# Loading the turned memory and the first key weights of a two-layer trunk in alternate pieces of 2, 2 and 4 chunks

## The chip, the cores and the metric

The kernel runs on one core of one Trainium2 chip. The metric is the device time of one launch in microseconds (us), lower is better. The trace comes from one execution under the hardware profiler; times of the trace are counted from the start of its span.

## The reference

A trunk of two layers over 256 rows of width 1024, all float32. Each layer runs a mixer (HGRN2, a short convolution and latent attention beside each other), a cross attention to a memory of 256 rows, and a mixture of 32 experts. Only the keys of the cross attention matter for the change:

```python
h = h + cross_attention(rms_norm(h, norm_cross[l]), rms_norm(mem, norm_mem[l]),
                        xa_wq[l], xa_wk[l], xa_wv[l], xa_wo[l])
# in cross_attention(h, m, wq, wk, wv, wo):
k = (m @ wk).reshape(B_, m.shape[1], XA_HEADS, XA_DIM)
v = (m @ wv).reshape(B_, m.shape[1], XA_HEADS, XA_DIM)
```

The product `m @ wk` sums over a width of 1024, which the kernel cuts into 8 chunks of 128 (KC = 8).

## The kernel before, in words

The first thing that the kernel computes is the keys and values of layer 0's cross attention, since they need only `mem` and weights. The weights come from HBM as units: `xk0` to `xk3` are the four quarters of `xa_wk`, `xv0` to `xv3` those of `xa_wv`, 1 MB each. All units go in a fixed order (RING_ORDER) through six ring buffers of 2 MB, `ring[0]` to `ring[5]`. SyncE (SP) issues every one of these loads from one queue. A unit's load is issued when TensorE has freed its buffer (`unit_free`), and its landing is counted on `unit_in[slot]`. At the start all six buffers are free. The order in which SP issues at the start is written out by hand (L572 to L584):

- half the turned memory (chunks 0 to 3, into `memN`, which lies in `early[5]`), half of `xk0` (chunks 0 to 3, into `ring[0]`), the other half of the memory, the other half of `xk0`, 512 KB each;
- `xk1`, `mem` in rows (into `kT`), the tables, `xk2`, `x`, the turned `x` (into `uT`), and then `xk3`, `xv0` and on.

VectorE multiplies the turned memory by the norm's gain, two chunks at a time, from `memN` into `mT` (L1811, four instructions, counted on `mem_gained`). The first and the third wait for a half of the memory (`memT_in`). The norm's row factors are put in later: ScalarE and VectorE compute them from `mem` in rows, and TensorE spreads them over the partitions (L921, `spread_rstd`) between `xk1` and `xk2`.

TensorE first runs WARM_UP = 10 products of zeros from `states` (L926), which depend on nothing that is loaded. Then come the keys of `xk0` (L937): for each of 8 chunks two products of 128 x 256, each of which the trace shows as two MATMUL records, so 32 in all. Chunk 0 waits for `part_in[0]` (the first half of `xk0`), chunk 4 for `unit_in[0]` (the second half), and every second chunk for `mem_gained`. `xk1`, `xk2` and `xk3` follow at once (`fill_keys`, L663), then the values (L722), then the mixer's projections.

The same semaphores `part_in[0]` to `part_in[2]` are used again much later, for the halves of the three last expert units of each layer (PARTED). The waits for them are at L799 and L869.

Much later the expert stages read 2 MB units from the ring and from the early buffers. There the loads run back to back and TensorE waits for some of them.

Of the kernel before, what the change touches and what calls it, by code (L numbers as in the profile page):

```python
# [28 lines left out]
P = 128  # L29
L = 2  # L30
S = 256
D = 1024
T = S // P
KC = D // P
# [16 lines left out]
RING = 6  # L51
UNIT = 4096
LEVELS = 4
WARM_UP = 10
LEAST_BLOCK = 8
UNIT_DMAS = 1
LOADED = 16 * UNIT_DMAS
# [26 lines left out]
UNIT_AT = [0]  # L84
# [207 lines left out]
def hybrid_trunk(nc, tables, level_masks, a, out):  # L292
    with ExitStack() as ctx:
        def sb(name, shape, dt=F32, stack=ctx):
            return stack.enter_context(nc.sbuf_tensor(name, shape, dt))

        def sem(name):
            return ctx.enter_context(nc.semaphore(name))


        ring = [sb(f"ring{n}", [P, UNIT]) for n in range(RING)]
# [3 lines left out]
        h = early[4][:, 0:T * D].rearrange("p (t d) -> p t d", t=T)  # L305
# [3 lines left out]
        memN = early[5][:, 0:KC * S].rearrange("p (c s) -> p c s", c=KC)  # L309
# [120 lines left out]
        unit_in = [sem(f"unit_in{n}") for n in range(RING)]  # L430
# [6 lines left out]
        memT_in = [sem(f"memT_in{n}") for n in range(2)]  # L437
        part_in = [sem(f"part_in{n}") for n in range(len(PARTED))]
# [29 lines left out]
        fixed_units = a["fixed_units"]  # L468
# [8 lines left out]
        def _(sp):  # L477
# [92 lines left out]
                    sp.dma_start(dst, src).then_inc(unit_in[slot], 16)  # L570

            sp.wait_ge(unit_free, 1)  # L572
            first = fixed_units[0, UNIT_AT[0]:UNIT_AT[1]].rearrange("(p h x) -> p h x", p=P, h=2)
            for n in range(2):
                half = slice(n * KC // 2 * S, (n + 1) * KC // 2 * S)
                sp.dma_start(memN.rearrange("p c s -> p (c s)")[:, half], a["mem_turned"][:, half]).then_inc(memT_in[n], 16)
                sp.dma_start(ring[0][:, half], first[:, n]).then_inc(part_in[0] if n == 0 else unit_in[0], 16)
            static_unit(0, 1)
            sp.dma_start(kT.rearrange("p c s -> p (c s)").rearrange("p (t d) -> p t d", t=T),
                         a["mem"].rearrange("b (t p) d -> p (b t) d", p=P)).then_inc(mem_in, 16)  # L580
# [37 lines left out]
        def _(pe):  # L618
# [29 lines left out]
            def wait_unit(base, name, of=None):  # L648
                wait_number(base, RING_AT[lay if of is None else of, name])
# [106 lines left out]
            def unit_memory(base, n, buffer, loads):  # L756

                if buffer is None:
                    if halved(n) is not None:
                        pe.wait_ge(half_in[halved(n)], LOADED * (lay + 1))  # L760
                    wait_number(base, n)
                    return ring[n % RING]
                pe.wait_ge(early_in[buffer], LOADED * loads)
                return early[buffer]

            def freed(buffer):
                return unit_free if buffer is None else early_free
# [59 lines left out]
            def down_view(unit):  # L827

                return unit.rearrange("p (h e c x) -> p e c h x", h=2, e=QUAD, c=2)
# [33 lines left out]
            def last_quarter(E, units, j):  # L863

                q = QUADS - 1
                number, buffer, loads = units[j // 2]
                w = down_view(unit_memory(None, number, buffer, loads))
                if j % 2:
                    pe.wait_ge(part_in[1 + j // 2], LOADED * (lay + 1))  # L869
                for c in range(2):  # L870
                    for e in range(QUAD):
                        mm = pe.matmul(bank[j % 2][32 * e:32 * e + 32, 0:S], turned[:, 2 + c, 32 * e:32 * e + 32], w[:, e, c, j % 2],
                                       start=(c == 0), stop=(c == 1), tile_position=(0, 32 * e))
                    if j == 2 and c == 0:
                        pe.wait_ge(E["m_down"], q * 2 + 2)
                        pe.sem_inc(freed(units[0][1]), 1)
                mm.then_inc(E["m_down"], 1)
# [14 lines left out]
            def last_down_and_scatter(E, units):  # L892

                pe.wait_ge(E["turned"], QUADS)
                last_quarter(E, units, 0)
                if lay == L - 1:
                    keep_busy(3, 4)
                last_quarter(E, units, 1)
                add_last_quarters(E, 0)
                if lay < L - 1:  # L900
                    last_quarter(E, units, 2)
                    add_last_quarters(E, 1)
                    last_quarter(E, units, 3)
                    add_last_quarters(E, 2)
                    add_last_quarters(E, 3)
                else:
                    last_quarter(E, units, 2)
                    add_last_quarters(E, 1)
                    last_quarter(E, units, 3)
                    for t in range(T):  # L910
                        for j in (2, 3):
                            add_last_quarter(E, j, t)
# [10 lines left out]
            lay = 0  # L923
            pe.wait_ge(setup_done, 1)
            for _ in range(WARM_UP):
                pe.matmul(bank[7][:, 0:P], states[:, 0, 0], states[:, 0, 1], start=True, stop=True)  # L926
            o = begin("xk0")
            w = slot_view("xk0")
            for c in range(KC):
                if c % 2 == 0:  # L930
                    pe.wait_ge(mem_gained, c // 2 + 1)
                if c == 0:
                    pe.wait_ge(part_in[0], LOADED)
                if c == KC // 2:
                    wait_unit(0, "xk0")
                for k in range(2):
                    mm = pe.matmul(o[:, k * S:(k + 1) * S], w[:, c, k * P:(k + 1) * P], mT[:, c], start=(c == 0 and k == 0),  # L937
                                   stop=(c == KC - 1), skip_group_check=True)
# [797 lines left out]
        def _(dve):  # L1736
# [68 lines left out]
            dve.memset(states[:, :, :, :], 0.0).then_inc(setup_done, 1)  # L1805
            dve.wait_ge(params_in, 16)
            for n in range(4):
                if n % 2 == 0:
                    dve.wait_ge(memT_in[n // 2], 16)
                first_gain = ptab[:, 0, PARAMS["gains"][0] + 2 * KC + 2 * n:PARAMS["gains"][0] + 2 * KC + 2 * n + 2]  # L1810
                dve.tensor_tensor(mT[:, 2 * n:2 * n + 2], memN[:, 2 * n:2 * n + 2],  # L1811
                                  first_gain.unsqueeze(2).broadcast_to([P, 2, S]), ALU.mult).then_inc(mem_gained, 1)
# [720 lines left out]
```

## Time and profile before

| | |
|---|---|
| device time, median of 3 runs | 899.73 us |
| lowest and highest of the 3 | 899.07 and 900.69 us |
| device time of the profiled execution | 902.04 us |
| its span | 900.2 us |
| TensorE busy | 843.3 us, 94% |
| TensorE's granted clock, mean over the span | 0.987 |
| HBM read | 270.76 MB |

The span is the time from the first to the last instruction of the profiled execution; its device time is 1.8 us longer. PE stands for TensorE's products, PEld for its weight loads, which run beside them, SPq for SyncE's queue. A granted clock of 1.00 is TensorE's 2.4 GHz, 0.50 is 1.2 GHz.

### The profile page before, as it was taken

Reading aid. Unit: us, or ns where it says so; the run is one execution under the profiler, and the core shown is the slowest. Engines: PE = TensorE matmul, PEld = TensorE weight load, DVE = VectorE, ACT = ScalarE, POOL = GpSimd, SP = SyncE. Lnnn points to the kernel's source line nnn. Section 1 sums busy time; section 2 is a strip of 40 time slices with the busy share of each in tenths; the row PEclk is TensorE's granted clock in tenths of the full one; section 3 lists DMA queues with packets and bytes.
Section 4 is the critical chain, followed back from the end, with each engine's and each line's share of the span. In section 5 each row is a group of like instructions: output and inputs, shape, how many; then the busy total and the mean of one; then the engine's idle time right before and its main releaser. Section 6 shows DMA issues by size and latency. Waiting matters only on the chain.

```text
span 900.2 us, 12111 instructions
## 1 busy us (share of the span) xinstructions
PE 843.3 (94%) x5188; PEld 564.8 (63%) x5188; DVE 275.1 (31%) x571; ACT 169.4 (19%) x399; POOL 15.0 (2%) x21
## 2 busy tenths in 40 slices
PE   8999999999999999989879999999999999877776
PEld 7888876679755655535527887766975644332333
DVE  2317557132234111101104674723122421110112
ACT  1211134411222000000012112451121200000003
POOL 0600000000000000000000000000000000000000
PEclk9999999999999999999999999999999999999899
DMA  9943555074678999999999445507766899999995
GB/s 348 390 171 132 188 187 187 12 302 162 272 283 339 427 424 429 426 428 425 426 422 380 150 156 194 204 1 272 312 280 226 341 428 424 428 427 427 427 422 234
DMA packets 25944, 272.64 MB, mean 303 GB/s; under 512 B 3232, under 2 KB 3616, under 8 KB 7200
## 3 DMA queue, kind: packets, MB, share of 16 engines
q1 hardware_dynamic: 24592, 270.52, 74.0%
q10 hardware_dynamic: 1296, 1.30, 0.5%
q8 instruction: 44, 0.72, 0.3%
q14 instruction: 12, 0.10, 0.0%
HBM read 270.76 MB, written 1.05 MB: 302 GB/s over the span
## 4 chain that ended last, share of the span: by engine, by line
PE 75%; DMA 20%; ACT 1%; SPq 1%; DVE 1%; issue 1%; another core or an unknown queue 0%; PEld 0%; DVEq 0%; PEldq 0%; ACTq 0%
DMA early<-in_expert_units 19%; PE bank L663 18%; PE bank L745 12%; PE bank L801 7%; PE bank L1165 6%; PE bank L775 4%; PE bank L841 3%; PE bank L722 3%; PE bank L853 3%; PE bank L730 2%; PE bank L1195 2%; PE bank L1176 2%; PE bank L984 2%; SPq L552 1%; PE bank L937 1%; PE bank L684 1%
## 5 line engine op out<-in xcount | busy, mean ns | idle before, releaser
L663 PE MATMUL bank<-uT,ring 128*128 128x256 f32 x480 | 107.0, 381 | 1.4 <-DVE uT L1786 0.8
L663 PEld LDWEIGHTS bank<-uT,ring 128*128 128x128 f32 x480 | 90.3, 190 | 15.2 <-issue 1.4
L801 PE MATMUL bank<-ring,xT 128*32 128x512 f32 x560 | 69.1, 630 | 17.7 <-DMA ring<-in_expert_units 17.5
L801 PE MATMUL bank<-early,xT 128*32 128x512 f32 x464 | 55.1, 610 | 15.4 <-DMA early<-in_expert_units 15.3
L1165 PEld LDWEIGHTS bank<-uT,ring 128*128 128x128 f32 x512 | 57.8, 192 | 1.1 <-DVE uT L1786 0.5
L1165 PE MATMUL bank<-uT,ring 128*128 128x128 f32 x512 | 57.8, 275 | 0.0
L745 PE MATMUL bank<-ring,early 128*128 128x512 f32 x128 | 56.6, 592 | 0.0
L801 PEld LDWEIGHTS bank<-ring,xT 128*32 128x32 f32 x560 | 17.5, 113 | 61.4 <-issue 43.9
L745 PE MATMUL bank<-ring,uT 128*128 128x512 f32 x128 | 55.9, 592 | 0.0
L853 PE MATMUL bank<-yy,states 128*128 128x512 f32 x112 | 54.1, 612 | 0.0
L2275 DVE TENSOR_TENSOR hid<-hid,bank 128x256 f32<-128x256 f32 x16 | 6.7, 421 | 150.1 <-ACT hid L1659 150.1
L775 PE MATMUL bank<-sel,hn 128*128 128x128 f32 x448 | 52.3, 275 | 0.0
L775 PEld LDWEIGHTS bank<-sel,hn 128*128 128x128 f32 x448 | 51.3, 192 | 0.5 <-issue 0.5
L801 PEld LDWEIGHTS bank<-early,xT 128*32 128x32 f32 x464 | 14.3, 111 | 53.4 <-issue 39.3
L1659 ACT ACTIVATE hid<-bank 128x256 f32<-128x256 f32 x16 | 6.1, 384 | 192.9 <-PE bank L801 192.9
L745 PEld LDWEIGHTS bank<-ring,uT 128*128 128x128 f32 x128 | 24.2, 190 | 27.9 <-issue 27.7
L745 PEld LDWEIGHTS bank<-ring,early 128*128 128x128 f32 x128 | 23.5, 190 | 25.8 <-issue 25.8
L2280 DVE COPY yy<-bank 128x512 f32<-128x512 f32 x14 | 9.7, 692 | 97.1 <-PE bank L841 97.1
L853 PEld LDWEIGHTS bank<-yy,states 128*128 128x128 f32 x112 | 19.5, 193 | 28.9 <-issue 27.7
L2254 DVE TENSOR_TENSOR xT<-bank,ptab 128x512 f32<-128x512 f32 x28 | 19.4, 691 | 45.6 <-PE bank L775 45.6
L841 PE MATMUL bank<-ring,states 128*32 128x512 f32 x256 | 29.3, 596 | 0.0
L841 PE MATMUL bank<-early,states 128*32 128x512 f32 x192 | 22.2, 596 | 2.5 <-DMA early<-in_expert_units 2.5
(328 smaller groups left out, 1034.0 us busy)
## 6 DMA issues: line engine op xcount, KB each, us to landing
ring<-in_expert_units SPq DMA_DIRECT2D x47, 2048.0 KB, 22.7
early<-in_expert_units SPq DMA_DIRECT2D x37, 2048.0 KB, 26.6
ring<-in_fixed_units SPq DMA_DIRECT2D x16, 2048.0 KB, 8.1
ring<-in_fixed_units SPq DMA_DIRECT2D x24, 1024.0 KB, 18.0
early<-in_expert_units SPq DMA_DIRECT2D x12, 1024.0 KB, 37.8
ring<-in_expert_units SPq DMA_DIRECT2D x8, 1024.0 KB, 6.3
early<-in_expert_units SPq DMA_DIRECT2D x8, 512.0 KB, 5.9
ring<-in_fixed_units SPq DMA_DIRECT2D x4, 512.0 KB, 5.3
```

Source lines behind the costliest of these rows:

```text
L663: mm = pe.matmul(o[row0:row0 + m], w[:, c, c0:c0 + m], rhs[:, c], start=(c == 0), stop=(c == chunks - 1))
L722: mm = pe.matmul(o[:, t * S:(t + 1) * S], mem[:, c, t * P:t * P + P], w[:, c], start=(c == 0), stop=(c == KC - 1))
L730: mm = pe.matmul(o[:, t * S:(t + 1) * S], mem[:, c, t * P:t * P + P], w[:, c], start=(c == 0), stop=(c == KC - 1))
L745: mm = pe.matmul(o[:, :], rows, w[:, c], start=(c == 0), stop=(c == KC - 1))
L775: mm = pe.matmul(bank[half][:, c * P:c * P + P], hn[:, t, half * 4 + c], sel[:, t].rearrange("p e s -> p (e s)"), start=(t == 0), stop=(t ...
L801: mm = pe.matmul(bank[2][32 * e:32 * e + 32, :], xT[:, 2 * n + c, 32 * e:32 * e + 32], w[:, e, :, c], start=(n == 0 and c == 0), stop=(n = ...
L841: mm = pe.matmul(bank[n][32 * e:32 * e + 32, :], turned[:, 2 + c, 32 * e:32 * e + 32], w[:, e, c], start=(c == 0), stop=(c == 1), tile_pos ...
L853: mm = pe.matmul(sums(t, n)[:, :], turned[:, 4 * odd + t], yy[:, n * 512:n * 512 + 512], start=False, stop=False, skip_group_check=True)
L984: mm = pe.matmul(o[:, t * S:(t + 1) * S], uT[:, c, t * P:t * P + P], w[:, c], start=(c == 0), stop=(c == KC - 1))
L1165: mm = pe.matmul(o[:, k * P:(k + 1) * P], w[:, c, k * P:(k + 1) * P], uT[:, c, t * P:t * P + P], start=(c == 0), stop=(c == KC - 1))
L1176: mm = pe.matmul(o[:, k * S:(k + 1) * S], qT[:, t, 2 * hx + c], kT[:, 2 * hx + c], start=(c == 0), stop=(c == 1))
L2254: dve.tensor_tensor(xT[:, 4 * half:4 * half + 4], bank[half][:, :].rearrange("p (c s) -> p c s", c=4), gains[:, 3, 4 * half:4 * half + 4]. ...
```

## The change

The memory and `xk0` are each cut into three pieces of 2, 2 and 4 chunks instead of two halves, still alternating and still from SP's one queue: six loads instead of four, of 256, 256, 256, 256, 512 and 512 KB. The landings are counted on `memT_in[0]`, `memT_in[1]` and `part_in[2]` for the memory, and on `part_in[0]`, `part_in[1]` and `unit_in[0]` for the weights. VectorE's multiplication waits ahead of chunks 0, 2 and 4, and TensorE's keys wait for weights ahead of chunks 0, 2 and 4. The warm-up has 7 products instead of 10. Since `part_in[1]` and `part_in[2]` are now each counted up once at the start, the wait at L869 asks for one load more.

```diff
-WARM_UP = 10
+WARM_UP = 7
+FIRST_PIECES = ((0, 2), (2, 4), (4, 8))
...
-            first = fixed_units[0, UNIT_AT[0]:UNIT_AT[1]].rearrange("(p h x) -> p h x", p=P, h=2)
-            for n in range(2):
-                half = slice(n * KC // 2 * S, (n + 1) * KC // 2 * S)
-                sp.dma_start(memN.rearrange("p c s -> p (c s)")[:, half], a["mem_turned"][:, half]).then_inc(memT_in[n], 16)
-                sp.dma_start(ring[0][:, half], first[:, n]).then_inc(part_in[0] if n == 0 else unit_in[0], 16)
+            first = fixed_units[0, UNIT_AT[0]:UNIT_AT[1]].rearrange("(p x) -> p x", p=P)
+            for n, (c0, c1) in enumerate(FIRST_PIECES):
+                piece = slice(c0 * S, c1 * S)
+                sp.dma_start(memN.rearrange("p c s -> p (c s)")[:, piece], a["mem_turned"][:, piece]).then_inc(part_in[2] if n == 2 else memT_in[n], 16)
+                sp.dma_start(ring[0][:, piece], first[:, piece]).then_inc(unit_in[0] if n == 2 else part_in[n], 16)
...
-                    pe.wait_ge(part_in[1 + j // 2], LOADED * (lay + 1))
+                    pe.wait_ge(part_in[1 + j // 2], LOADED * (lay + 2))
...
-                if c == 0:
-                    pe.wait_ge(part_in[0], LOADED)
+                if c < KC // 2 and c % 2 == 0:
+                    pe.wait_ge(part_in[c // 2], LOADED)
...
-                if n % 2 == 0:
-                    dve.wait_ge(memT_in[n // 2], 16)
+                if n < 2:
+                    dve.wait_ge(memT_in[n], 16)
+                if n == 2:
+                    dve.wait_ge(part_in[2], 16)
```

## Rows read from the trace of the kernel before

**Rows 1.** The page: busy time of TensorE, and TensorE and DMA in 40 slices.

```profile
PE 843.3 (94%) x5188; PEld 564.8 (63%) x5188; DVE 275.1 (31%) x571; ACT 169.4 (19%) x399; POOL 15.0 (2%) x21
...
PE   8999999999999999989879999999999999877776
...
DMA  9943555074678999999999445507766899999995
```

**Rows 2.** The chain that ended last: start, us, what.

```profile
1.32 7.04 DMA ring<-in_fixed_units
...
8.50 8.83 PE bank L937 x32
17.33 6.91 PE bank L663 x32
24.24 0.43 PE bank L921 x2
...
373.57 39.19 DMA early<-in_expert_units
```

**Rows 3.** Stretches: width, busy us (records) of PE, PEld, DVE, ACT, POOL; PE's clock; DMA share, GB/s.

```profile
1.70:6.40 4.70, 4.63 (x20) 4.34 (x20) 1.29 (x2) 0.73 (x1) 0.00 (x0) 1.00 0.89 283
6.40:8.50 2.10, 0.00 (x0) 0.03 (x1) 0.00 (x0) 0.00 (x0) 0.00 (x0) 1.00 0.88 308
8.50:9.90 1.40, 1.40 (x7) 1.25 (x8) 0.00 (x0) 0.00 (x0) 0.00 (x0) 1.00 1.04 427
9.90:13.30 3.40, 3.40 (x10) 2.69 (x9) 2.52 (x12) 0.20 (x1) 0.00 (x0) 0.50 1.01 418
13.30:17.30 4.00, 4.00 (x20) 3.54 (x19) 0.19 (x2) 0.00 (x0) 0.00 (x0) 1.00 1.03 426
```

**Rows 4.** Timeline, SP's issues at the start: start, us, what.

```profile
0.88 0.38 SPq L576 DMA_DIRECT2D early<-in_mem_turned  x1
...
1.32 0.42 SPq L577 DMA_DIRECT2D ring<-in_fixed_units  x1
...
1.78 0.43 SPq L576 DMA_DIRECT2D early<-in_mem_turned  x1
2.26 0.43 SPq L577 DMA_DIRECT2D ring<-in_fixed_units  x1
2.73 0.61 SPq L542 DMA_DIRECT2D ring<-in_fixed_units  x1
```

**Rows 5.** From issue to landing, by line: the memory's two halves, then xk0's two.

```profile
L576 SPq DMA_DIRECT2D early<-in_mem_turned x2: 381/406/432, 0.9 to 1.8; - x2
...
DMA to landing us min/median/max: 4.0/6.2/8.5
...
L577 SPq DMA_DIRECT2D ring<-in_fixed_units x2: 420/426/432, 1.3 to 2.3; - x2
...
DMA to landing us min/median/max: 7.0/8.2/9.3
```

**Rows 6.** From issue to landing: the load of xk1, issued at 2.73.

```profile
L542 SPq DMA_DIRECT2D ring<-in_fixed_units x1: 612/612/612, 2.7 to 2.7; - x1
...
DMA to landing us min/median/max: 11.3/11.3/11.3
```

**Rows 7.** Timeline of VectorE: the gains, and the row factors' diagonals that L921 reads.

```profile
5.01 1.29 DVE L1811 TENSOR_TENSOR mT<-early,ptab 128x512 f32<-128x512 f32 x2 [3.34 <-DMA early<-in_mem_turned]
10.28 1.29 DVE L1811 TENSOR_TENSOR mT<-early,ptab 128x512 f32<-128x512 f32 x2 [3.98 <-DMA early<-in_mem_turned]
...
21.24 0.48 DVE L1854 TENSOR_SCALAR mV<-tab,mem_rs 128x128 f32<-128x128 f32 x2
```

**Rows 8.** By line: records of the warm-up, and the same shape at L917 (ns: min/median/max).

```profile
L926 PE MATMUL bank<-states x20: 421/421/581, 1.7 to 5.9; 128*128 128x128 f32 x20
...
L917 PE MATMUL bank<-tab x56: 275/275/377, 271.4 to 885.6; 128*128 128x128 f32 x56
```

**Rows 9.** Who waited for whom on SP's queue: us in total, times, longest.

```profile
SPq L542 <- PEq L754: 429.9, 39, 32.3
```

## The prediction on record

> **What bounds the kernel now.** I read the page first: TensorE is busy for 94% of the span, so the kernel is bound by TensorE outside the expert stages [rows 1]. The change touches only the first 17 us, so the question is what sets TensorE's course there, and whether what it gains is still there at the end.
>
> The chain of waits answers the first part. It begins with the first half of `xk0`, issued at 1.32 and landed at 1.32 + 7.04 = 8.36; the keys of `xk0` start at 8.50, take 8.83 us and end at 17.33; `xk1` follows without a gap and takes 6.91 us [rows 2]. `xk0` and `xk1` are the same work, 32 records of one shape. So there are two losses: a wait (the warm-up's 20 records fill 1.7 to 6.4, then TensorE stands for 2.1 us [rows 3]) and 8.83 - 6.91 = 1.92 us in the products. The stretches say what the second is: the clock is granted at 1.00 until 9.9, at 0.50 (1.2 GHz) from 9.9 to 13.3, and at 1.00 again [rows 3]. It fell behind the idle stretch of 2.1 us and rose behind 3.4 us of unbroken work. No load stopped the products in the middle: the second half of `xk0` landed at 2.26 + 9.3 = 11.56 [rows 4, 5], and the 17th record, the first that needs it, starts only about 13 (7 + 10 records run up to 13.3 [rows 3]).
>
> When do the loads land? Memory half one at 0.88 + 4.0 = 4.9, `xk0` half one at 8.36, memory half two at 1.78 + 8.5 = 10.28, `xk0` half two at 11.56, `xk1` at 2.73 + 11.3 = 14.0 [rows 4 to 6]. Each half is 512 KB, so by 4.9 us 512 KB are complete, by 8.36 1 MB, by 10.28 1.5 MB, by 11.56 2 MB. The DMA engines carry 308 GB/s up to 8.5 and 418 to 427 after [rows 3]: from 8.5 on the loads, not their issue, are the limit.
>
> **The change part by part.** *The first pieces.* Memory and `xk0`, chunks 0 and 1, are together the first 512 KB, as the memory's first half was. They land together at about 4.9, the memory's 256 KB earlier, and its gain (1.29 / 2 = 0.65 us [rows 7]) is then done about when the weights land. The keys start at 4.9 + 0.14 = 5.0 instead of 8.50 (0.14 is 8.50 - 8.36).
>
> *The warm-up.* Ten products take 4.63 us, so seven take 3.24 us and end at 1.72 + 3.24 = 4.96: TensorE is free just as the first piece lands. With ten it would have been held until 6.36. The warm-up's records took 421 ns where the same shape takes 275 ns later [rows 8], so it ran at the lower clock although the page's clock shows 1.00 there. I expect the first key records to be slow too. Eight records cost 6.91 / 4 = 1.73 us at full clock. The half-clock stretch of 3.4 us held about eight and cost 1.92 us more, so eight slow ones cost at most 1.73 + 1.92 = 3.65 us. Chunks 0 and 1 thus end between 6.7 and 8.65. What comes next lands at 8.36, so this term costs 0 to 0.3 us; I take 0. The cover is the second piece's landing: were it gone, the slow clock would cost up to 1.9 us.
>
> *The second pieces.* With them 1 MB has been asked for, as before with `xk0`'s first half, so they land at 8.36; the memory's part is earlier and its gain is hidden. Chunks 2 and 3 run from 8.5 to 10.23. TensorE stands before that for 0 to 1.8 us.
>
> *The third pieces.* The memory's last 512 KB land at 10.28 and their gains are done at 10.93 and 11.57, as now [rows 7]. The weights' last 512 KB land at 11.56. Chunks 4 to 7 run from 11.7 for 6.91 / 2 = 3.46 us and end at 15.2. TensorE stands before that for 11.7 - 10.23 = 1.5 us.
>
> *The size of the pieces.* No row shows a load of 256 KB at this place. At the rate of the nearest rows (256 KB at 418 GB/s) four small pieces cost what two halves did, 0 us extra. The upper bound is that a small piece takes as long as a half, 11.56 - 10.28 = 1.28 us: 2 x 1.28 = 2.56 us more. I take 0.1 us, near the lower end, since the halves already land 1.3 to 1.9 us apart while their issues are 0.45 us apart [rows 4], so the cost that one load has from issue to landing is shared and not added.
>
> The Trainium skill (DMA: Bandwidth & Descriptors, Anatomy of one DMA) gives a fit of 2.0 us fixed plus the bytes at 436 GB/s for one DMA, and calls most of the fixed part completion. If that part were paid one after another, two more loads would cost 4 us and the change would lose; the rows above have 512 KB landing 1.28 us after the last, which is less than the fixed part by itself, so the trace says that it overlaps.
>
> *SP's two more issues.* Each takes about 0.47 us from start to start [rows 4], so all that stands behind them on SP (`xk1`, `mem` in rows, tables, `xk2`, `x`, turned `x`, `xk3`) is issued 0.94 us later, `xk1` at 3.67. The first bytes of `xk1` can't move before `xk0` is through, and from 8.5 on the DMA engines are full [rows 3]; the cover is that queue, and the cost is 0. Without it, it would be 0.94 us.
>
> *VectorE.* One more wait, ahead of the second gain. Behind it stand only the gains and the small work on the table of lower bounds; it waits for nothing later than now. 0 us. *The later waits* on `part_in` count one load more for one load more: 0 us.
>
> **The sum.** In the profiled execution the keys of `xk0` end at 15.2 + 0.1 = 15.3 instead of 17.33: 2.0 us, of which 1.9 is the clock that stays up and 0.1 the landings (8.50 + 6.91 = 15.4 would be today's end without the fall).
>
> Does it stay? `xk1` landed at 14.0, ahead of 15.3. The next work with another input is L921 at 24.24, which would come at 22.2; its diagonals are done at 21.24 + 0.48 = 21.72 [rows 2, 7], 0.5 us early. That is what is late next: it caps the gain at 24.24 - 21.8 = 2.4 us. Behind that TensorE goes on without a gap, and SP's loads wait for buffers that TensorE frees (429.9 us in 39 waits [rows 9]), so they move with it. The waits of the expert stages for loads, as the 39.19 us from 373.57 [rows 2], belong to streams that begin when TensorE frees buffers, and so move too. The span would be 900.2 - 2.0 = 898.2.
>
> That is one execution, and its own time is 902.04 against a median of 899.73. Whether the clock falls behind a gap of 2.1 us is the main part of the sum, and one trace shows it once. The three runs spread over 1.62 us, nearly the size of that term, which is what it would look like if some executions paid it and others not. So for the median I count the clock at half: 0.96 + 0.1 = 1.1 us, 898.6.
>
> The Trainium skill (TensorE: Matmul & The Clock Gate, What's actually happening) says the same of the clock from another side: where it changes varies from run to run with the phase at the kernel's start. No run here shows it yet. By it the half is right, without it the full 2.0.
>
> **Rivals.**
> *The fall is paid in every run before.* For it: the only trace has it. Against it: the spread. Then the full 2.0 us are gained: 897.7.
> *Nothing is left.* The fall is rarely paid unprofiled, or the slowest part of the last piece is what matters either way: the keys end at 15.4 before and 15.3 after. 899.6. For it: without the fall both ends rest on landings 0.1 us apart in effect.
> *The clock falls after the change.* There are two new pauses of up to 1.8 and 1.5 us in place of one of 2.1. For it: the fall came behind a pause hardly longer. Against it: chunks 2 and 3 lie between them. It costs 1.9 us on top of 1.1 gained: 900.5.
> *Small pieces cost as much as large ones* (the slower side). The last weights land at 11.56 + 2.56 = 14.1; TensorE stands from 10.2 to 14.3, longer than the pause that brought the clock down, and chunks 4 to 7 take 3.46 + 1.92. The end is 19.6 instead of 17.33, and 3.2 us are lost against a median that pays the clock half the time: 902.9. It loses against the median once the last piece lands about 1 us later than 11.6, that is from 0.5 us extra for a pair of small pieces. No row shows such a price, and none excludes it.
>
> **How the numbers follow.** What a measurement can tell from no change is about 0.2%, 1.8 us. Half the clock term 0.47 (898.6; own range 897.9 to 899.4), the full term 0.23 (897.7), nothing left 0.17 (899.6), a fall after the change 0.07 (900.5), small pieces dear 0.06 (902.9). The range from 897.3 (the cap of 2.4 us) to 900.2 holds the first three, and leaves out the last two with some of the edges. Faster by over 0.2% means below 897.9: most of the full term and a little of the first, 0.27. Slower means above 901.5: 0.06. The rest, 0.67, is the same.
>
> **What would show it.** After the change: the warm-up's 14 records end near 5.0; the first L937 record starts near 5.1 and the first eight are slow; a pause ends at about 8.4 and one at 11.6, both for `ring<-in_fixed_units`; the clock stays at 1.00 from 8 to 17; L663 starts near 15.3; L921 near 22.2. The prediction is wrong if the first piece lands much after 5, if the third lands after 12, if the clock falls behind one of the pauses, or if TensorE stands before L921.

## The result, and the profile after

The change makes the kernel a little slower. The median is 901.66 us (22 runs, 899.57 to 904.53) against 899.98 us for the kernel before (22 runs, 898.99 to 916.91). The ratio is 1.0015 with a 95% interval of 1.0009 to 1.0022: about 1.4 us lost (0.0015 x 900; the medians themselves are 1.7 us apart), less than the 0.2% named in the prediction, but a loss where it forecast 1.1 us gained. The single 916.91 us of before counts as a slow execution, which the ratio leaves out. The profiled execution took 901.59 us, its span is 899.8 us.

The page of the kernel after, in the lines that answer to [rows 1]. The work is the same (PE 843.8 us busy against 843.3), and the DMA slices differ at the start and hardly after it.

```profile
PE 843.8 (94%) x5182; PEld 564.0 (63%) x5182; DVE 275.3 (31%) x571; ACT 169.3 (19%) x399; POOL 14.0 (2%) x21
...
PE   8999999999999999989889999999999999786786
...
DMA  9953455073679999999999445507766899999995
```

The timeline of TensorE and VectorE of the kernel after (start, us, what, and in brackets the idle time before it and what ended it):

```profile
1.72 3.36 PE L927 MATMUL bank<-states 128*128 128x128 f32 x14 [1.72 <-DVE states L1806]
5.22 3.01 PE L938 MATMUL bank<-mT,ring 128*128 128x256 f32 x8
9.31 1.96 PE L938 MATMUL bank<-mT,ring 128*128 128x256 f32 x8 [1.08 <-DMA ring<-in_fixed_units]
12.15 3.69 PE L938 MATMUL bank<-mT,ring 128*128 128x256 f32 x16 [0.88 <-DVE mT L1814]
...
10.75 1.30 DVE L1814 TENSOR_TENSOR mT<-early,ptab 128x512 f32<-128x512 f32 x2 [4.30 <-DMA early<-in_mem_turned]
```

The warm-up ends at 5.08 and the keys start at 5.22, as forecast. Then each piece is late. The second eight records start at 9.31 (forecast 8.5) and the last sixteen at 12.15 (forecast 11.7). The keys end at 12.15 + 3.69 = 15.85. That is still earlier than the 17.33 of [rows 2], in an execution whose span is 0.4 us shorter than that of before. By these two traces alone the change would look like a small gain. The chain of the kernel after (start, us, what) names the memory's last load and, behind it, VectorE's gain. The weights' last load lands at the same time (12.0):

```profile
3.06 7.67 DMA early<-in_mem_turned
10.75 1.31 DVE mT L1814 x2
12.15 3.69 PE bank L938 x16
15.85 6.91 PE bank L664 x32
22.75 0.43 PE bank L922 x2
```

The loads, by line, as in [rows 5]: the three pieces of `xk0` from issue to landing, the last 3.53 + 8.5 = 12.0.

```profile
L578 SPq DMA_DIRECT2D ring<-in_fixed_units x3: 422/432/759, 1.3 to 3.5; - x3
...
DMA to landing us min/median/max: 3.7/6.9/8.5
```

### The profile page after: what moved, and what is told of

It reads as the page before. It is cut to its first block, busy times and chain, and to the rows that moved or that the text cites. A ratio compares the mean times of both kernels' runs of the same rounds, so it can differ in the third digit from the quotient of the medians.

```text
span 899.8 us, 12102 instructions
## 1 busy us (share of the span) xinstructions
PE 843.8 (94%) x5182; PEld 564.0 (63%) x5182; DVE 275.3 (31%) x571; ACT 169.3 (19%) x399; POOL 14.0 (2%) x21
## 4 chain that ended last, share of the span: by engine, by line
PE 75%; DMA 20%; ACT 2%; DVE 1%; issue 1%; SPq 1%; another core or an unknown queue 0%; PEld 0%; DVEq 0%; PEldq 0%; ACTq 0%
DMA early<-in_expert_units 19%; PE bank L664 18%; PE bank L746 12%; PE bank L802 7%; PE bank L1166 6%; PE bank L842 3%; PE bank L776 3%; PE bank L723 3%; PE bank L854 3%; PE bank L731 2%; PE bank L1196 2%; PE bank L1177 2%; PE bank L985 2%; PE bank L685 1%; PE bank L873 1%
## 5 line engine op out<-in xcount | busy, mean ns | idle before, releaser
L802 PEld LDWEIGHTS bank<-ring,xT 128*32 128x32 f32 x560 | 17.5, 113 | 61.6 <-issue 44.0
L746 PEld LDWEIGHTS bank<-ring,uT 128*128 128x128 f32 x128 | 24.2, 190 | 27.9 <-issue 27.7
L842 PE MATMUL bank<-ring,states 128*32 128x512 f32 x256 | 29.3, 596 | 0.0
L842 PE MATMUL bank<-early,states 128*32 128x512 f32 x192 | 22.2, 596 | 3.9 <-DMA early<-in_expert_units 3.9
```

Of the source, the lines that this page charges most:

```text
L746: mm = pe.matmul(o[:, :], rows, w[:, c], start=(c == 0), stop=(c == KC - 1))
L802: mm = pe.matmul(bank[2][32 * e:32 * e + 32, :], xT[:, 2 * n + c, 32 * e:32 * e + 32], w[:, e, :, c], start=(n == 0 and c == 0), stop=(n = ...
L842: mm = pe.matmul(bank[n][32 * e:32 * e + 32, :], turned[:, 2 + c, 32 * e:32 * e + 32], w[:, e, c], start=(c == 0), stop=(c == 1), tile_pos ...
```

## A second look at the kernel before

The traces and the times point in opposite directions, so the unchanged kernel before was profiled once more. (It was made after most of the runs below, and stands first because they are read against it.)

> A second profile of the kernel before, for its start. If its first trace (the first half of xk0 landed at 8.4, the clock fell, the keys ended at 17.3) was an unusual execution: landed at 6.0 to 6.6, no fall, keys ended at 13.5, and TensorE waits for xk3 at about 28. If it was usual: as in the first trace within 1 us.

It took 899.15 us, its span is 897.4. The timeline of TensorE, and the chain that ended last:

```profile
1.72 3.96 PE L926 MATMUL bank<-states 128*128 128x128 f32 x20 [1.72 <-DVE states L1805]
6.36 7.22 PE L937 MATMUL bank<-mT,ring 128*128 128x256 f32 x32 [0.68 <-DVE mT L1811]
```

```profile
0.88 4.07 DMA early<-in_mem_turned
5.06 1.31 DVE mT L1811 x2
6.36 7.22 PE bank L937 x32
13.59 6.91 PE bank L663 x32
20.50 0.43 PE bank L921 x2
20.93 13.92 PE bank L663 x64
```

And its loads of `xk0`, by line:

```profile
L577 SPq DMA_DIRECT2D ring<-in_fixed_units x2: 420/426/432, 1.3 to 2.3; - x2
...
DMA to landing us min/median/max: 4.9/6.2/7.5
```

The kernel is the same as in [rows 2], the start is another one. The warm-up ends at 1.72 + 3.96 = 5.68. The first half of `xk0` lands at 1.32 + 4.9 = 6.2, not 8.36, and TensorE starts the keys at 6.36, the 0.14 us behind the landing that [rows 2] shows too (the profile puts the wait down to VectorE, whose first gain was done by about 5.7). The pause is 0.68 us instead of 2.1, the clock does not fall behind it, and the keys end at 13.59 instead of 17.33. Against this execution the changed kernel is 15.85 - 13.59 = 2.3 us late at the end of the keys of `xk0`.

## The experiments

**The parts one by one.** First, each half of the change alone, and the changed kernel once more.

```diff
 # pieces only: the changed kernel with
-WARM_UP = 7
+WARM_UP = 10
 # warm-up only: the kernel before with
-WARM_UP = 10
+WARM_UP = 7
```

> The six loads and their waits, with the ten warm-up products of before. Theory A (the pieces bring the loss, by something behind the start): about 901.4, as the changed kernel, with its wider spread. Theory B (the shorter warm-up brings the loss, since the key products then begin at half clock or with more idle time): about 900.0, as before or 0.2 below. The first key record starts at 6.5 and keys end at 15.3 in either case.

> The kernel before with 7 warm-up products instead of 10: TensorE then stands from 5.0 to 8.5 instead of from 6.4. Theory A: as before, 900.0. Theory B: slower by about 1.4 us. If the clock now starts the keys at half speed every time, 32 records cost up to 1.9 us more than at full clock; that is what before paid in its one trace too, so theory A allows 0 to 1 us.

> The changed kernel once more, for a second profile and its spread beside the others of this job. Both theories: ratio 1.0015, about 901.4, single times from 899.6 to 904.5. Open: whether the keys of xk0 end at 15.8 again (then the spread arises later) or between 14 and 19 (then at the start).

Pieces alone: 900.99 us, ratio 1.0009 [0.9998, 1.0020]. Warm-up alone: 899.85 us, 0.9999 [0.9990, 1.0008]. The changed kernel again: 902.02 us, 1.0017 [1.0008, 1.0027]. So three products fewer do nothing that can be measured, and the loss belongs to the pieces. By this run alone the interval of the pieces reaches 1; the next run and the cut kernels below add to it.

**The pieces' loads without their early start.** The six loads stay, with ten warm-up products, but TensorE starts the keys only when the first four chunks are there, as before.

```diff
-                if c < KC // 2 and c % 2 == 0:
-                    pe.wait_ge(part_in[c // 2], LOADED)
+                if c == 0:
+                    pe.wait_ge(part_in[0], LOADED)
+                    pe.wait_ge(part_in[1], LOADED)
```

> Six loads and ten warm-up products, but TensorE's chunk 0 waits for both small weight pieces, so that the keys start only with the second piece at about 8.4 to 9.3, as before. Theory A1 (the loads themselves, cut finer, cost time later): about 901.4. Theory A2 (the pauses between the pieces bring the clock down in some executions): 900.0, since there is one pause again.

It took 903.37 us, 1.0033 [1.0017, 1.0048]. The timeline:

```profile
10.52 8.57 PE L939 MATMUL bank<-mT,ring 128*128 128x256 f32 x32 [4.17 <-DMA ring<-in_fixed_units]
```

The first 1 MB is there only at 10.4 us; in the two traces of the kernel before it was at 8.4 and 6.2. Behind the pause of 4.17 us the clock is granted at 0.50 from 11 to 13 us, and the 32 records take 8.57 us instead of 6.91, so in this execution 1.66 us is the clock's. Two things cost here, the late landing and the clock that falls behind the wait for it; the early start of the change avoids the second.

**Which loads are dear?** Three other ways to cut. Pieces of 4, 2 and 2 chunks have the small loads last; pieces of 2 and 6 have two small loads first, and four loads in all; the third keeps four whole chunks in a load, but takes the first half of memory and of weights as two loads of 64 partitions each, which makes six loads with long rows.

```diff
 # 4, 2 and 2 chunks, with a warm-up of 10 and the waits moved to chunks 0, 4 and 6
+FIRST_PIECES = ((0, 4), (4, 6), (6, 8))
 # 2 and 6 chunks, in the kernel before, with the waits moved to chunks 0 and 2
+            for n, (c0, c1) in enumerate(((0, 2), (2, 8))):
 # six loads by rows, in the kernel before, with the waits counting both loads of a half
+                for p0, p1 in ((0, 64), (64, 128)) if n == 0 else ((0, 128),):
```

> Six loads, cut 4, 2, 2 instead of 2, 2, 4, with ten warm-up products: the start is as before, only the tail is finer. Theory P (small pieces slow the first 2 MB down, wherever they stand): the first half lands as before, at 6.3 to 8.4, and the last piece later than before but ahead of its use, so the keys end where the first half puts them: 900.0 to 900.5. Theory C (six loads instead of four cost time whatever is waited for, by SP's issues): about 901.4. Theory W (the waits for later pieces do it, since chunks 4 to 7 begin only with the last piece): as before, 900.0.

> Four loads as before, but cut 2 and 6 chunks (256 and 768 KB each), ten warm-up products. Chunk 2 now waits for the last piece. Theory W: the last weights land at 9.6 to 11.5, six chunks take 5.2 us, so the keys end at 15 to 17 against 13.3 to 15.4 in executions of before without a straggling DMA engine: slower by about 1.5 us, 901.6. Theory P alone (only small rows cost): two small loads instead of four, about 0.5 us later plus the same wait, 901 to 902. Theory C: no further load, so as before, 900.0.

> The first half of the memory and of the weights each as two loads of 64 partitions, rows of 4 KB as before, and the waits as before: six loads, but the same rows and row sizes. Beside the run with six loads of 2 KB rows and the same single wait (1.0033). If the number of loads is what delays the first MB: about 903. If the size and number of rows is: about 900.0.

4-2-2: 900.42 us, 0.9998 [0.9986, 1.0010]. 2-6: 902.05 us, 1.0021 [1.0012, 1.0030]. Six by rows: 904.42 us, 1.0042 [1.0028, 1.0056]; here too the keys start late (9.62) and the clock is at 0.50 from 9 to 15 us, so its time is not the price of the loads alone. The stretch from 5 to 8 us in four kernels (the last figure is GB/s), first before (its second look):

```profile
5.00:8.00 3.00, 2.32 (x15) 1.98 (x14) 1.29 (x2) 0.00 (x0) 0.00 (x0) 1.00 0.91 335
```

After:

```profile
5.00:8.00 3.00, 2.85 (x9) 2.19 (x8) 0.86 (x2) 0.00 (x0) 0.00 (x0) 1.00 0.85 203
```

Pieces of 4, 2 and 2:

```profile
5.00:8.00 3.00, 2.39 (x13) 2.09 (x12) 1.29 (x2) 0.00 (x0) 0.00 (x0) 1.00 1.00 324
```

Six loads by rows:

```profile
5.00:8.00 3.00, 0.93 (x7) 0.73 (x5) 1.00 (x2) 0.00 (x0) 0.00 (x0) 1.00 0.89 198
```

The DMA engines are marked as busy 85 to 100% in these four rows; what they carry differs. Where four small loads lead, whether cut by chunks or by partitions, they carry about 200 GB/s in these rows. Where two halves lead, or one half and then small ones, they carry over 320 in these rows. This speaks against the length of a row as the cause (the loads by partitions have the rows of a half) and for the four small loads at the head. But each of the two controls is one or two executions, and the loads by partitions differ in one more thing: each takes SyncE 0.57 to 0.60 us to issue instead of 0.43.

The table has one line for each shape, from the same view and from the landings by line. Profiles of kernels with another warm-up, with other waits and of the cut kernels further down are counted with their shape.

| shape of the loads | executions profiled | last of `xk0` lands, us | GB/s, 5 to 8 us |
|---|---|---|---|
| two halves | 9 | 9.6 to 11.6, median 10.0 | 266 to 341 |
| 4, 2, 2 | 2 | 10.2, 10.5 | 324, 247 |
| 2, 6 | 1 | 10.6 | 317 |
| 2, 2, 4 (the change) | 7 | 10.6 to 13.0, median 12.0 | 172 to 227, once 279 |
| six, by rows | 1 | 12.4 | 198 |

The change lands the weights 2.0 us later by the medians. The two ranges overlap: one execution with the change's pieces has 10.6 and 279 GB/s, another lands at 11.0, and the first trace of before has 11.6. The 247 GB/s of one execution of 4, 2 and 2 is nearer to the change than to its own other one.

The engines' busy share is not as high everywhere: in three other executions with the change's pieces it is 0.72, 0.77 and 0.79 over the same stretch, at 200, 172 and 223 GB/s. SyncE shows a sign of its own there. The issue of `mem` in rows on SyncE's queue, after, in the second look at before, and in the one execution with 279 GB/s:

```profile
4.48 1.41 SPq L580 DMA_DIRECT2D kT<-in_mem  x1
```

```profile
3.42 0.48 SPq L579 DMA_DIRECT2D kT<-in_mem  x1
```

```profile
4.31 0.47 SPq L580 DMA_DIRECT2D kT<-in_mem  x1
```

In the seven executions with four small loads ahead and 172 to 227 GB/s, this issue or that of the tables takes 1.3 to 1.9 us; in the eighth none of SyncE's issues ahead of that of `xk3` takes over 0.7; with two halves the longest of these is 1.1. Whether SyncE is held up by the slow loads or the loads by SyncE, no run here settles.

The pieces of 2 and 6 show the second cost. Their loads land early, and they still lose. The timeline:

```profile
6.00 1.89 PE L937 MATMUL bank<-mT,ring 128*128 128x256 f32 x8
10.68 5.42 PE L937 MATMUL bank<-mT,ring 128*128 128x256 f32 x24 [2.79 <-DVE mT L1811]
```

The early start runs eight records, then TensorE stands for 2.8 us for everything else, and 24 records of 5.42 us follow the last landing; the keys end at 16.1. With two halves, as in the second look at before, half of the work is already behind TensorE when the last load lands, and the keys run through with 0.3 us lost at most (7.22 against 6.91 us). The pause of 2.79 us here brings no fall of the clock (1.00 in the stretches from 5 to 13 us), where one of 2.1 us did in [rows 3]: the length of a pause alone does not tell whether the clock falls.

**How much of a start comes through?** A pure delay, with no load touched: the kernel before with longer warm-ups.

```diff
-WARM_UP = 10
+WARM_UP = 24
```

> The kernel before with 24 warm-up products instead of 10: at 0.46 us each while slow and 0.28 us after, they end about 10.5, so the keys start there instead of at 6.4 to 8.5, with the clock up. This measures how much of a later start reaches the end. Full passage: slower by 2 to 4 us, 902 to 904. If the expert stages' loads are what sets the end and their stream does not move with TensorE: 900 to 901.

> The kernel before with 24 warm-up products once more. In the cut it was 1.6 us slower, in the first full run level (interval from 0.999 to 1.001). If a later start passes to the end in full: 1.001 to 1.0025, the first run was at the edge of its interval. If something later gives it back: 1.000 again.

> The kernel before with 38 warm-up products: the keys start at about 12.8 instead of 6.4, the keys of xk3 at about 34 instead of 27.7 to 28.5, so 5.5 to 6 us later. Full passage: 1.006 to 1.0067. If the expert stages' loads absorb part: clearly less, and the two warm-up runs give the share.

24 products: 900.54 us, 1.0000 [0.999, 1.001], and on another occasion 901.17 us, 1.0010 [1.0000, 1.0019]. 38 products: 905.04 us (5 runs), 1.0044 [1.0029, 1.0058]. The chain of the last:

```profile
1.72 11.39 PE bank L926 x76
13.11 6.91 PE bank L937 x32
20.02 6.91 PE bank L663 x32
27.36 13.81 PE bank L663 x64
```

The keys of `xk3` start at 27.36 + 6.91 = 34.3, some 6.4 us late against 20.93 + 6.91 = 27.8 in the second look at before, and 0.0044 x 900 = 4.0 us of it are left at the end, about 60% (40 to 80% by the interval). Part of it is given back at the first long wait for expert weights. In the chain (where the load waited for begins, and its us), the second look at before, then 24 products (the second run), then 38:

```profile
369.94 38.77 DMA early<-in_expert_units
408.75 1.92 PE bank L841 x16
```

```profile
373.40 37.76 DMA early<-in_expert_units
411.21 1.92 PE bank L841 x16
```

```profile
376.26 37.72 DMA early<-in_expert_units
414.03 1.92 PE bank L841 x16
```

The load is issued 3.5 and 6.3 us later and is waited for 2.5 and 5.3 us later: 1 us is given back in each. The changed kernel gives back nothing there:

```profile
372.08 39.03 DMA early<-in_expert_units
411.16 1.92 PE bank L842 x16
```

It comes 2.1 us late and leaves 2.4 us late. Nor does the first trace of before, which is as late as the 24 products (373.57 [rows 2]): it leaves at 373.57 + 39.19 = 412.8, 4.0 us late. So lateness alone does not decide what is given back there.

**The start by itself.** Since whole executions scatter by some us, the start was timed alone: the kernels cut off behind the keys of `xk3`. All that follows (both layers and the output) is left out; `x` is written out as it came, so the result is not that of the trunk.

```diff
 # TensorE, behind the keys of xk3; ScalarE and VectorE ahead of the layer loops;
 # SyncE behind the first loads, waits for all of them, and the store of x
+        return
 # GpSimd: in the first four cuts behind the angles, in the last three already ahead of the tables
+        return
```

> The kernel before, cut off behind the keys of xk3 (TensorE's course ends there, all first loads are waited for, x is written out as it came; the rest of the computation is left out). In the trace of before this point was 38.5 us, so some 45 to 50 us in all. This is the yardstick for the three others of this job; its spread tells how far the start alone varies.

> The same cut of the changed kernel. Theory S (the loss of 1.4 us arises at the start, since the last piece lands late and chunks 4 to 7 wait for it): 1 to 2 us above the cut of before. Theory L (the start gains or is level, and the loss arises later): level or up to 2 us below it.

> The same cut of the kernel with pieces of 4, 2 and 2 chunks. Theory S: level with the cut of before within 0.5 us, since the first half decides both. Theory L: no statement.

> The same cut of the kernel with pieces of 2, 2 and 4 chunks and ten warm-up products. Theory S: as the cut of the changed kernel within 0.3 us, since the warm-up's end is hidden behind the second piece. If the shorter warm-up matters, the two differ by up to 1.9 us through the clock.

> The cut of the kernel before behind the keys of xk3, now with GpSimd's chain on the positions left out too, since in the first cuts that chain ended last in the fastest executions and set a floor. Everything behind the keys of xk3 is left out. Yardstick; expected 40 to 42 us, with the keys of xk3 starting at 28 to 31.

> The same cut of the changed kernel. If the whole loss arises at the start: 1.0 to 1.8 us above the cut of before, since xk3 lands about 1.2 us later and the keys of xk0 end about 1.5 us later. If half of it arises later, as the first cuts (0.7 us) say at face value: 0.5 to 0.8 us.

> The same cut of the kernel with 24 warm-up products: its keys start at about 9.1 whatever the loads do, and those of xk3 at 30.2. Beside it the cut of before tells where a usual execution of before lies. If before pays a late landing or a fall of the clock in most executions (31.4 in its trace): this one is level or up to 1 us faster. If before's trace was an unusual one (27.9 and 28.3 in two like it): this one is 1 to 2 us slower, and the missing loss of the full kernel with 24 products has another cause later.

| cut of | median us | range | runs |
|---|---|---|---|
| before (s1) | 41.80 | 41.34 to 42.20 | 6 |
| before (c1) | 41.80 | 41.25 to 42.19 | 6 |
| after (s2) | 42.49 | 42.14 to 44.32 | 7 |
| after (c2) | 44.23 | 41.76 to 44.69 | 6 |
| pieces, warm-up 10 (s4) | 42.45 | 41.95 to 43.79 | 6 |
| pieces 4-2-2 (s3) | 42.32 | 41.98 to 44.11 | 6 |
| before, warm-up 24 (c3) | 43.42 | 43.10 to 44.60 | 6 |

The twelve executions of before lie within 1 us, with a mean of 41.75. The thirteen of after lie in two groups, seven near 42.3 (0.6 us above before) and six near 44.3 (2.6 us above), with a mean of 43.25: +1.5 us. Both profiled executions of after are of the upper group.

The cuts do not tell the shapes apart: 4-2-2 is 0.5 us above before by the median and 0.8 by the mean (one of six at 44.1), pieces with ten warm-up products 0.65 and 0.8. That 4, 2 and 2 costs nothing rests on the whole kernel alone (0.9998 [0.9986, 1.0010]). The first four cuts have a floor, since GpSimd's chain on the positions ended last in one of them; that is why the cut was repeated without it. Pieces with 7 and with 10 warm-up products do not differ by the median (42.49 and 42.45). The chain of the repeated cut of after:

```profile
9.44 21.70 DMA ring<-in_fixed_units
31.18 7.17 PE bank L674 x32
```

Here the keys of `xk3` wait for their load, which lands at 31.1. In the second look at before TensorE reaches them at 27.8 while the load lands at 5.97 + 21.7 = 27.7. Warm-up alone (7 products) shows the same wait in the whole kernel:

```profile
6.01 21.86 DMA ring<-in_fixed_units
27.92 7.17 PE bank L663 x32
```

So `xk3` lands just as TensorE comes to it. It lands 17.5 to 18.7 us behind the last weights of `xk0` in every profiled execution, so the lateness of the first loads is handed on by it, even where the keys of `xk0` would have left TensorE early.

**The scatter of single executions.** The profiled pieces-only execution took 905.36 us against its median of 900.99. Its stretch at the end of layer 0's experts, and the same of the second look at before:

```profile
470.10:480.00 9.90, 9.21 (x76) 4.46 (x74) 0.42 (x1) 3.77 (x8) 0.00 (x0) 0.65 1.02 428
```

```profile
470.10:480.00 9.90, 9.21 (x70) 6.45 (x63) 2.83 (x10) 3.62 (x13) 0.00 (x0) 1.00 1.01 423
```

The granted clock is 0.65 in one and 1.00 in the other. From the end of the long wait (L841 or L842) to the first 26 records of L730 or L731 it is 70.9 us against 68.5, and 69.2 in the changed kernel (clock 0.76). This belongs to the execution: the changed kernel's second profile has 68.6.

## Why the prediction was wrong

Its forecast was 898.6 us (1.1 us gained), measured was a loss of about 1.4 us. Step by step:

*What was right.* The first pieces land at 5.0 and the keys start at 5.22 (forecast 5.0), though one cut has them at 6.3 and 6.4. The warm-up's seven products end at 5.08 (4.96). The first eight key records are slow and take 3.01 us, inside the 1.73 to 3.65 given. The clock does not fall behind the two new pauses of 1.08 and 0.88 us. TensorE does not stand at L921, and 7 against 10 products make no difference by themselves.

*The step that failed first: "there are two losses", a wait and a fall of the clock.* Both were read from one execution and all later durations were set against it. Of nine profiled executions with two halves, the first half of `xk0` lands between 6.0 and 7.1 us in seven, at 7.9 in one and at 8.4 in the first trace. In none of the other eight is the clock granted below 1.00 before 22 us, and in the second look at before the keys end at 13.59, not 17.33. (In one cut the first key records are still slow and the 32 take 7.91 us, 1.0 more than at full clock.) The prediction doubted the clock term and counted it at half. It did not doubt the landing of 8.36, on which the pause, the clock term and the second pieces' time all stood. The sign was there: it says that the halves land 1.3 to 1.9 us apart, but its own landings of 4.9 and 8.36 are 3.5 apart; in the second look at before they are 1.3 apart. With that landing at 6.2 there is little to gain: the keys can't end before 5.2 + 6.9 = 12.1 even if every piece is there, and what was to be gained is 1.5 us at best. The Trainium skill (TensorE: Matmul & The Clock Gate, What's actually happening) has the clock's changes vary with the phase at the kernel's start; these runs agree that it varies: with two halves the one fall of the clock came in the execution whose load landed latest, behind a pause of 2.1 us, and the pause of 2.79 us with pieces of 2 and 6 brought none.

*The step that failed second: "the size of the pieces", 0.1 us.* It measures 2.0 us (medians of the last landing, 12.0 against 10.0), within the bounds of 0 to 2.56 and at the upper end. The argument for the lower end was that issue-to-landing times overlap, by rows of 512 KB loads. They do overlap, but the rate falls while four small loads lead. Why less is carried there is not settled. The fit that the prediction quotes beside this term (the Trainium skill, DMA: Bandwidth & Descriptors, Anatomy of one DMA) is given there for DMAs issued from GpSimd, while SyncE issues these; no sum rests on it.

*The cover that was missed.* With two halves, the last landing (10.0) is hidden behind the first sixteen records (from 6.4 to about 10). With 2, 2 and 4 the last sixteen start only behind it and behind its gain: 12.0, then 3.69 us. So 2.0 us more in the landing became 15.85 - 13.59 = 2.3 us at the end of the keys.

*"SP's two more issues", at 0.* `xk1` is issued at 4.01 (forecast 3.67) and `xk3` at 8.85 instead of 7.34, 1.5 us later and not 0.94. By itself this costs nothing that the traces show, since `xk3` lands 17.5 us behind the last weights of `xk0` in both traces. Whether it has a part in the slower loads is the open question above.

*"That is what is late next".* Not L921, but the load of `xk3`, whose landing at 27.7 meets TensorE at 27.8. Where the first loads land as usual it limits a gain at the start to nearly nothing, and it moves with them.

*"Does it stay?"* Taken as yes. A pure delay comes through at about 60% (38 products, 40 to 80% by the interval). For the change, +1.5 us in the mean of the cuts stand against 1.4 us in the whole. At 60% these would give 0.9 us. The intervals (0.8 to 2.0 us for the whole kernel) allow that, and the changed kernel gave nothing back at layer 0's long wait in its two profiles, so it may also be all. This stays open.

The rival *small pieces cost as much as large ones* had the right mechanism and nearly the right price of a piece. It had 0.06, and its 902.9 was worked out from the same late landings and a fall of the clock, which no profile of the changed kernel showed.

## What to carry to other kernels

Profile a kernel's start more than once before you count on a pause in it: one execution in nine here had a pause of 2.1 us and a fall of the clock that the others had not, and the median of the times said nothing about it. When first loads are cut finer to start sooner, two things are to be set against the early start: what the extra loads do to the last landing, and how much work is left behind it. Where half the work was already hidden ahead of the last landing, the finer cut had nothing to win, and a later load (here `xk3`) held any gain at the start back.

## What the runs showed that was not expected

Four loads of 256 KB at the head of the queue, cut either way, brought the rate in the stretch from 5 to 8 us to 172 to 227 GB/s in seven of eight executions, against 266 to 341 with two halves. Two small ones ahead (317) or small ones behind a half (324, 247) did not show it as clearly. The cause is open: the DMA engines' busy share was 0.85 or more in the rows shown, but down to 0.72 in others, and SyncE's issues took up to 1.9 us there. With two halves, the second load in the queue (the first half of `xk0`) lands between 6.0 and 8.4 us, from one execution to the next. The profile's clock reads 1.00 in the first microseconds while the warm-up's records take 421 ns, as in [rows 8], in every run. In one cut of the 4, 2 and 2 pieces the records are slow until 11 us, and the 32 of `xk0` take 8.72 us with no 0.50 in the profile's clock. And a delay of the start by 1.6 us (24 products, by the cut) could hardly be measured at the end of the whole kernel: 1.0000 and 1.0010.
